# A third block's rounded weights in a place of their own, ahead of the up projection of a hybrid decoder step

## The reference, cut to what matters

```python
def conv_ffn(x, buf, w_up, conv_w, conv_b, w_down):
    h_gate, h_val = jnp.split(x @ w_up, 2, axis=-1)
    hc, new_buf = causal_dwconv(h_gate, buf, conv_w)
    return (jax.nn.silu(hc + conv_b) * h_val) @ w_down, new_buf

# for each layer l
h = h + gt_m * rmsnorm(out, p['norm_g'][l, 1])              # behind the token mixer
u = rmsnorm(h, p['norm_g'][l, 2]) * (1 + sc_f) + sh_f       # ahead of the channel mixer
out, nb = conv_ffn(u, st_conv_f[l], p['ffn_w_up'][l], ...)
```

## Time and profile before

| | us |
|---|---|
| median of 3 runs | 3021.64 |
| lowest, highest | 3018.35, 3023.63 |
| span of the profiled execution, first to last instruction | 3014.3 |
| PE busy in it | 2876.1 (95%) |
| DVE, ACT, POOL busy in it | 1528.4, 1085.0, 1321.5 |

### The profile page before, as it was taken

One profiled execution on the slowest core, in us unless ns is written; L12 is line 12 of the kernel. 1 busy time (PEld: TensorE's weight loads), 2 busy tenths in 40 slices (PEclk: granted clock), 3 DMA queues, 4 the chain that ended last, 5 costly groups with the idle time before them and its releaser, 6 DMA issues.

```text
span 3014.3 us, 72962 instructions
## 1 busy us (share of the span) xinstructions
PE 2876.1 (95%) x29617; PEld 2733.3 (91%) x29617; DVE 1528.4 (51%) x2080; ACT 1085.0 (36%) x2139; POOL 1321.5 (44%) x959
## 2 busy tenths in 40 slices
PE   6999999998989999999998999999999999899998
PEld 5998999997978877899997899889999899799998
DVE  3435666118357874666603242476650444566612
ACT  4224333225455652433323444343332422433322
POOL 3443444442435554344443273434444344344443
PEclk9999999999999999999999999999999999899999
DMA  7544333544411013333354323533334543133332
GB/s 269 164 151 159 95 92 88 158 128 136 119 44 32 4 37 124 120 89 92 99 159 152 99 64 112 169 123 89 92 116 146 173 120 91 57 92 92 91 91 85
DMA packets 465618, 332.56 MB, mean 110 GB/s; under 512 B 19914, under 2 KB 435608, under 8 KB 465122
## 3 DMA queue, kind: packets, MB, share of 16 engines
q1 hardware_dynamic: 461400, 325.24, 35.1%
q10 hardware_dynamic: 4010, 4.22, 0.6%
HBM read 319.62 MB, written 10.20 MB: 109 GB/s over the span
## 4 chain that ended last, share of the span: by engine, by line
PE 62%; DVE 4%; ACT 2%; issue 1%; DMA 1%; SPq 0%; POOL 0%; ACTq 0%; DVEq 0%
PE banks L1667 33%; PE banks L1675 16%; PE banks L2126 5%; PE banks L2133 1%; PE banks L1628 1%; PE banks L1973 1%; DVE h L2662 1%; PE banks L1690 1%; DVE proj L2606 1%; PE banks L1761 0%; DMA s_state<-in_state_wkv_b_dram 0%; ACT conv L1080 0%; PE banks L2135 0%; ACT uv L1433 0%; DVE proj_b L2606 0%
## 5 line engine op out<-in xcount | busy, mean ns | idle before, releaser
L765 POOL TENSOR_TENSOR w_lo<-w_raw,w_hi 128x1024 fp32r<-128x1024 f32 x395 | 1007.5, 2551 | 1108.1 <-ACT w_hi L981 1088.0
L1667 PE MATMUL banks<-u_hi,w_hi 128*128 128x260 f32 x4064 | 834.5, 287 | 14.2 <-ACT w_hi L981 9.4
L1667 PE MATMUL banks<-u_lo,w_hi 128*128 128x260 f32 x4064 | 825.1, 284 | 0.0
L1667 PEld LDWEIGHTS banks<-u_hi,w_hi 128*128 128x128 f32 x4064 | 627.4, 189 | 27.1 <-issue 15.2
L1667 PEld LDWEIGHTS banks<-u_lo,w_hi 128*128 128x128 f32 x4064 | 629.9, 189 | 1.6
L981 ACT ACTIVATE w_hi<-w_raw 128x1024 fp32r<-128x1024 f32 x402 | 424.5, 1056 | 454.2 <-PE banks L1675 284.4
L1675 PE MATMUL banks<-u_hi,w_lo 128*128 128x260 f32 x4064 | 527.5, 282 | 0.0
L1675 PEld LDWEIGHTS banks<-u_hi,w_lo 128*128 128x128 f32 x4064 | 502.1, 187 | 1.3
L1667 PE MATMUL banks<-hid_hi,w_hi 128*128 128x260 f32 x1664 | 336.3, 283 | 0.0
L1667 PE MATMUL banks<-hid_lo,w_hi 128*128 128x260 f32 x1664 | 335.2, 283 | 0.0
L3113 DVE TENSOR_TENSOR csb<-proj 128x520 f32 (+1 forms) x42 | 30.3, 722 | 470.8 <-ACT proj L1048 470.8
(11 more groups left out here) (463 smaller groups left out, 3898.8 us busy)
## 6 DMA issues: line engine op xcount, KB each, us to landing
w_raw<-in_ffn_w_up_dram SPq DMA_DIRECT2D x176, 512.0 KB, 3.7
ada_raw<-in_ada_w_dram SPq DMA_DIRECT2D x96, 512.0 KB, 4.7
w_raw<-in_ffn_w_down_dram SPq DMA_DIRECT2D x64, 448.0 KB, 3.7
w_raw<-in_sconv_w_in_dram SPq DMA_DIRECT2D x48, 512.0 KB, 5.2
ada_ahead<-in_ada_w_dram SPq DMA_DIRECT2D x36, 512.0 KB, 7.7
ada_ahead_down<-in_ada_w_dram SPq DMA_DIRECT2D x36, 512.0 KB, 6.2
w_raw<-in_ffn_w_down_dram SPq DMA_DIRECT2D x32, 512.0 KB, 4.0
ada_pro<-in_ada_w_dram SPq DMA_DIRECT2D x6, 2048.0 KB, 21.2
```

The lines of the kernel that those rows point to most:

```text
L765: pool.tensor_tensor(w_lo[:, s, :, :], w_raw[:, s, :, :], w_hi[:, s, :, :].bitcast(F32), ALU.subtract).then_inc(lo_done, 1)
L1667: pe.matmul(tile_ps[slot][half][0:width, 0:HALF], w_hi[:, s, k, 0:width], x[:, k0 + k, half * HALF:(half + 1) * HALF], start=start and k = ...
```

## The change

The rounded part of the up projection's third block (block `n0 + 2`, the second unit's gate) goes to a place of its own, `third_hi`, instead of slot 0 of `w_hi`. So its rounding need not wait until the first pair has been multiplied: ACT does it in the norm behind the mixer, right behind the second block's rounding. There it waits for the third block's load (`w_loaded[0]`). PE multiplies the third block with `third_hi`; the transposes of the first unit's tail and of the second unit's state move from ahead of this block into it, between its 32 and its 16 matmuls. The load of the Silu table moves behind the first gate's copies. POOL makes the third block's rest from `third_hi`, once the first pair is done (`low_third`). On ACT and POOL the loop's first round is written out.

```diff
--- before.py
+++ after.py
@@ -230,6 +230,7 @@
         wa2 = at("wa2", [8, 2, GH * P], F32, half_off + 2 * T * 4)
         shift_rows = at("shift_rows", [NSEQ, D], F32, big_off + 3 * slab_bytes)
         shift_in = at("shift_in", [NS, D], F32, half_off)
+        third_hi = at("third_hi", [P, KT, P], F32R, big_off + 37440)
         ahead_at = {0: [big_off + 62400 + i * 4 * ADA_W for i in range(6)],
                     2: [big_off + 3 * slab_bytes + 8192 + i * 4 * ADA_W for i in range(6)],
                     "down": [u_off + slab_bytes + i * 4 * ADA_W for i in range(4)]
@@ -765,6 +766,13 @@
                 pool.tensor_tensor(w_lo[:, s, :, :], w_raw[:, s, :, :], w_hi[:, s, :, :].bitcast(F32),
                                    ALU.subtract).then_inc(lo_done, 1)
 
+            def low_third(n):
+
+                pool.wait_ge(hi_done, n + 1)
+                pool.wait_ge(block_done, n + 1)
+                pool.tensor_tensor(w_lo[:, 0, :, :], w_raw[:, 0, :, :], third_hi[:, :, :].bitcast(F32),
+                                   ALU.subtract).then_inc(lo_done, 1)
+
             def low_parts(n, s):
 
                 pool.wait_ge(hi_done, n + 1)
@@ -941,7 +949,11 @@
                         if ahead:
                             low(n0 + 4 * it + 2 * e + 3, 1)
 
-                    with pool.Fori(0, p["iters"] - 1) as it:
+                    tails(q0, 0, gate_ready)
+                    low_third(n0 + 2)
+                    low(n0 + 3, 1)
+                    hidden_tile(0, 1, True)
+                    with pool.Fori(1, p["iters"] - 1) as it:
                         hidden_tile(it, 0, True)
                         hidden_tile(it, 1, True)
                     hidden_tile(p["iters"] - 1, 0, True)
@@ -1087,6 +1099,9 @@
                     if n0 < NBLK:
                         half_of = lambda _n: n0 // 2
                         high(n0 + 1, 1)
+                    if p["sub"] == 1:
+                        act.wait_ge(w_loaded[0], 16 * (n0 // 2 + 1) + 16)
+                        act.activation(third_hi[:, :, :], w_raw[:, 0, :, :], ACT.Copy).then_inc(hi_done, 1)
                 elif p["kind"] == "sconv":
                     j = l // 3
 
@@ -1521,9 +1536,7 @@
                     out_pair(p["iters"] - 1, True)
                 elif p["kind"] == "up":
 
-                    act.activation(warm[:, :], eps_col[:, :], ACT.Silu)
-
-                    def hidden_tile(it, e, ahead):
+                    def hidden_tile(it, e, ahead, first=False):
 
                         nonlocal half_of
                         n, q, m = n0 + 4 * it + 2 * e, q0 + 2 * it + e, 2 * it + e
@@ -1538,7 +1551,10 @@
                         act.wait_ge(gate_ready, q + 1)
                         act.sem_inc(tile_free[0], 1)
                         half_of = lambda _n: n0 // 2 + 2 * it + e + 1
-                        high(n + 2, 0)
+                        if first:
+                            act.activation(warm[:, :], eps_col[:, :], ACT.Silu)
+                        else:
+                            high(n + 2, 0)
                         act.wait_ge(conv_done, q + 3)
                         act.activation(conv[:, e, 0:CWD], conv[:, e, 0:CWD], ACT.Silu,
                                        bias=vec("ffn_conv_b", l * FT + m)).then_inc(silu_done, 1)
@@ -1548,7 +1564,9 @@
                                      O["conv_ffn_prompt"][l, 0, :, ds(m * P, P)],
                                      O["conv_ffn_sample"][l, :, 1, ds(m * P, P)])
 
-                    with act.Fori(0, p["iters"] - 1) as it:
+                    hidden_tile(0, 0, True, True)
+                    hidden_tile(0, 1, True)
+                    with act.Fori(1, p["iters"] - 1) as it:
                         hidden_tile(it, 0, True)
                         hidden_tile(it, 1, True)
                     hidden_tile(p["iters"] - 1, 0, True)
@@ -1656,15 +1674,16 @@
                     pe.wait_ge(ada_pro_loaded[i % KT], 16 * (2 * (h - 2) + i // KT + 2))
                     ada_columns(ahead_of(h)[i % KT][:, :], i % KT)
 
-            def gemm(n, s, slot, xh, xl, k0, nk, start, stop, ready=None, width=P, between=None):
+            def gemm(n, s, slot, xh, xl, k0, nk, start, stop, ready=None, width=P, between=None, high=None):
 
                 pe.wait_ge(hi_done, n + 1)
+                stationary = w_hi[:, s] if high is None else high
                 for k in range(nk):
                     if ready is not None:
                         pe.wait_ge(ready[0], ready[1] + k + 1)
                     for i, x in enumerate((xh, xl)):
                         for half in range(2):
-                            pe.matmul(tile_ps[slot][half][0:width, 0:HALF], w_hi[:, s, k, 0:width],
+                            pe.matmul(tile_ps[slot][half][0:width, 0:HALF], stationary[:, k, 0:width],
                                       x[:, k0 + k, half * HALF:(half + 1) * HALF],
                                       start=start and k == 0 and i == 0, stop=False)
                 if between is not None:
@@ -2445,14 +2464,23 @@
                             pe.wait_ge(tile_free[0], t0 // 2 + 1)
                             pe.wait_ge(tile_free[1], t0 // 2 + 1)
                             gemm_pair(n0, p["pre"], u_hi, u_lo, (u_ready, KT * (p["split"] - 1)))
-                        else:
-                            for part in range(2):
-                                pe.wait_ge(tile_free[part], t0 // 2 + 2 * it + e + 1)
-                                gemm(n0 + 4 * it + 2 * e + part, part, part, u_hi, u_lo, 0, KT, True, True)
+                            return
+                        for part in range(2):
+                            pe.wait_ge(tile_free[part], t0 // 2 + 2 * it + e + 1)
+                            gemm(n0 + 4 * it + 2 * e + part, part, part, u_hi, u_lo, 0, KT, True, True)
                         turn_tail(q, e)
 
+                    def second_states():
+
+                        turn_tail(q0, 0)
+                        turn_state(q0 + 1, q0 // 2, 1)
+
                     hidden_tile(0, 0, True)
-                    hidden_tile(0, 1)
+                    pe.wait_ge(tile_free[0], t0 // 2 + 2)
+                    gemm(n0 + 2, 0, 0, u_hi, u_lo, 0, KT, True, True, between=second_states, high=third_hi)
+                    pe.wait_ge(tile_free[1], t0 // 2 + 2)
+                    gemm(n0 + 3, 1, 1, u_hi, u_lo, 0, KT, True, True)
+                    turn_tail(q0 + 1, 1)
                     with pe.Fori(1, p["iters"]) as it:
                         for e in range(2):
                             hidden_tile(it, e)
```

## The result

The changed kernel takes 3039.32 us (median of 6 runs, 3038.09 to 3048.40); the kernel before, measured beside it, takes 3019.42 (6 runs, 3015.76 to 3023.63). The ratio is 1.0071, with a 95% interval of 1.0060 to 1.0082: slower, by about 20 us. The forecast was 3046, its range 3036 to 3060.

The account below looks back on a forecast made before the run. PE, busy 2876.1 of 3014.3 us, was taken as the bound, so its idle and half clock decide. 31.3 + 1.5 - 4.8 - 3.4 = +24.6 us gave span 3038.9 and time 3046 us, range 3036 to 3060.

Parts of the forecast that it names:

- The wait: Norm ahead of up, layers 0 to 2: rounding waits for its load ahead of the squares, delaying the root; +31.3 us.
- The clock behind the root: Layers 0 to 2, spreading or first pair after the root: part may run at half clock; 0.5 a layer, +1.5 us.
- The rival of a clock that stays low through the first pair: Layers 0 to 2: idle leaves PE at half clock into the pair; some 3059 us, chance 0.15.
- the rival with the load in time: Third block's weights land when ACT is free, so no wait; four starts gain 8.2 us: 3013 us, chance 0.04.
- The gap: PE idle between first pair and third block shrinks: 1.3 us in layers 0 to 2, 0.9 in layer 3; -4.8.
- Hidden by 0.2 us only: Up start: fourth block's wait for the first unit's product stays covered by 0.2 us; otherwise a few tenths per layer.
- Layer 3: Its third-block load lands some 3.7 us after issue, before the first square, so the wait costs nothing there.
- The half clock behind the gap: Third block's beginning, two of four layers: half clock gone with the shorter gap; -3.4 us.
- The median: Whole kernel: forecast span 3038.9, with the earlier median's 7.3 us above its span added, gives 3046 us.

Follow-up runs that it names:

- the wait alone: Kernel before plus ACT waiting for the third block's load where the change rounds it, nothing rounded early: 3045.28 us against 3017.74, ratio 1.0088.
- the earlier load: Changed kernel with SP issuing the third block's load ahead of the eight `ada_w` loads: 3013.65 us, ratio to the kernel before 0.9984.
- the rounding behind the root: Changed kernel with the third block's rounding moved behind the root of the norm ahead of the channel mixer, load unmoved: 3009.45 us, ratio 0.9971.
- without the own place: Changed kernel with the third block rounded into slot 0 behind the pair again, ahead of the table's load, transposes still inside the block: 3022.27 us.
- the rest in its own place: Changed kernel with the third block's load issued earlier, plus POOL making the block's rest in `third_lo` behind the root: 3011.01 us, ratio to before 0.9976.
- the second execution: The changed kernel run once more, unchanged: 3046.73 us, against 3017.67 for the kernel before beside it.
- the table alone: Kernel before with only the Silu table's load moved, behind the third block's rounding: 3016.86 us, one run.

## Why the prediction was right

**The wait** was the largest term and decided the sign. It was put at +31.3 us of root delay; the table gives 9.05 + 12.98 + 9.82 = 31.9, and the wait alone, in the kernel before, loses 27.5 us in the end; the earlier load wins 31.6 back in the four places and some 26 in the whole kernel. Two errors cancel in it: the squares could begin 1.3 us sooner in sum than I had them (the load landed 9.0 us behind its issue in layer 0, not 10.0), and from square to root it took 8.0, 9.4 and 8.5 us, where I had 8.0 in each and 9.3 as the upper bound. The 9.4 is layer 1, whose sums stay longest at the half clock.

**The clock behind the root.** The size agrees by luck: +1.5 predicted, +1.65 found (+1.3 with a pair that is 0.35 us shorter), but all of it in layer 1, where the `ada_w` columns behind the root run at the half clock. The kernel with the rounding behind the root and the one without the own place show the same 6.33 us in the same layer, and neither has the long idle ahead of it. So no run shows that the idle caused this part. First a round of layer 1, then of layer 0:

```profile
1250.48 1.93 PE L1646 MATMUL banks<-ada_ahead,cT 128*32 128x256 f32 x16
```

```profile
285.93 1.07 PE L1646 MATMUL banks<-ada_ahead,cT 128*32 128x256 f32 x16
```

What the long idle does show is the low clock of the sums. The clock that falls over an idle stretch agrees with what the Trainium skill says (TensorE: Matmul & The Clock Gate, "What's actually happening"): 0.65 over the 11.8 idle us, then 0.50 under work.

**The rival of a clock that stays low through the first pair** is wrong: PE is at 0.81 in the mean before the root already, and the pair takes 12.1 us in layers 0 and 2, as it did. Of the rival with the load in time, the mechanism was right, only not for this kernel: with the load ahead there is no wait, and the time is 3013.65 us. That it had 3013 is luck: it took 8.2 us off 3021.64, and the gain measured against the kernel before beside it is 4.1 us (3017.74 to 3013.65).

**The gap** was put at -4.8 us and the half clock behind it at -3.4, together -8.2. From the pair's end to the fourth block it was 9.75, 9.76, 8.24 and 7.81 us and is 6.98 in each: -7.65; the fourth block is 0.08 longer in each, which leaves -7.3. Within this the gap is shorter than I had it (0.63, not 0.9 to 1.0: the gate's copies begin at 299.80, ahead of the end of the pair's last products at 300.01), and the third block longer: 6.35, not 6.0.

**"Hidden by 0.2 us only"**, of the fourth block behind the first product, is the step that failed. The product ends 6.2 us behind the gate's copies, as it did (6.13). But the third block begins 0.1 us behind them, not 0.3, and its own 6.06 us then end ahead of product and signal. I had also counted no signal: the fourth block starts 0.23 us behind the product's end. It costs 0.3 us a layer. That the product is no sooner, though nothing stands ahead of DVE, has the cause that the kernel with the rest in its own place shows: one of DVE's three steps always runs beside POOL's rest. In the kernel before it was the third one; DVE and POOL there:

```profile
292.43 2.65 DVE L2578 SCALAR_TENSOR_TENSOR conv<-gate,vecs,conv 128x536 f32<-128x536 f32 x1 [0.15 <-DVE conv L2576]
```

```profile
292.08 2.43 POOL L765 TENSOR_TENSOR w_lo<-w_raw,w_hi 128x1024 fp32r<-128x1024 f32 x1 [0.68 <-ACT w_hi L981]
```

**Layer 3** was to be free and is: 2.3 us shorter than before. Only some 0.8 of this belongs to the gap and the blocks behind it. The root is 0.8 us earlier and the pair 0.7 shorter, which I had not forecast; the root repeats in the second execution, the pair doesn't (14.45 us), and this layer is then 0.85 us shorter than before. So it is in part luck that the four places come to +24.3 us where the sum had +24.6; in the second execution they come to +26.6.

**The half clock behind the gap** went in both layers, as predicted, but my reason was too simple. Over all executions it followed none of the 28 gaps of 0.63 to 1.56 us. Of the gaps of 1.9 to 2.4 us it followed 2 of 4 in the kernel before, the same two when repeated, 2 of 4 without the own place, and none with the wait alone or the table alone. It repeats within a kernel and is not set by the gap's length. What sets it stays open.

**The median** came out 6.7 us below the 3046. By the spans the step is +22.9 where my sum was +24.6, which is 1.7 of it. The rest, 5 us, is the way from the span to the time: I added 7.3 us, the distance of the first median from the span shown. But the changed kernel's profiled execution took 3038.95 us, 1.75 more than its span, and the kernel before, profiled once more, took 3017.32, 2.1 more than its span of 3015.2; so most of the 7.3 was that the execution shown of before happened to be a short one. That was no property of the kernel and should not have been carried over in full. By the medians the step is +19.9 us, and in the later pair of single runs +29.1 (3046.73 against 3017.67), so the scatter of executions is as large as this miss. The upper end of the forecast's own range, 3056, was also not its bounds' sum: 3014.3 + 39.2 + 7.3 is 3060.8.

## What to carry to other kernels

Before an instruction is moved forward in an in-order queue, look up two things in the trace: when the data that it waits for lands, and what stands behind it in the queue. Here a 1 us rounding was moved in front of the squares that all of the next stage hangs on, while its load stood behind eight others; the same rounding behind the root, or the same load eight places earlier, took the loss away and made the kernel 0.1 to 0.3% faster than before instead of 0.7% slower. And a gap of which several pieces are to go is worth only what the next limit allows: of 1.8 us of gap in layer 2, 1.3 came out, since the product of another engine set the start of the block after.

## What the runs showed of the hardware

- A DVE step of 128x536 with three operands took 0.78 us alone and 2.65 or 2.82 us beside a subtraction on POOL that had begun 0.35 or 0.14 us sooner. In both cases it ended 0.57 us behind POOL's end (295.08 against 294.51, 304.17 against 303.60). The kernel before has 208 such steps. 102 of them lasted 2.64 to 2.99 us, and all of these ran beside POOL's rest and ended 0.57 to 0.58 us behind its end; the other 106 took 0.78, most of them begun 0.3 to 0.6 us ahead of POOL's instruction. That is a step held up until POOL is done, not one that runs at a lower rate. The Trainium skill says so (SBUF — State Buffer, "SBUF: two separate sides"): the two share a port pair as an exclusive lock, which a DVE operation with two on-chip inputs needs against a GpSimd operation that reads there. If all of the step's 0.78 us came behind the lock, it would end 0.78 us behind POOL, which is an estimate; here it was 0.57.
- The Silu table's load took 1.28 us (300.64 to 301.92 in the changed kernel); ACT stood idle 0.10 us ahead of it, and the next ACT instruction stood 0.01 us behind it.
- A load of 512 KB behind eight others landed 8.9 to 10.0 us after its issue, in layers 0 to 2 of the kernel before and of the changed one. With nothing ahead of it, in layer 3 of the kernel before, the same load took 3.7 us, which is also the median of all 176. While it was under way in layer 0 of the changed kernel, the DMA engines were at 0.97 and moved 357 GB/s.
- The half clock came without a long idle too. In layer 1 of the kernel without the own place, eight sums took 0.44 us at 1222.78 (0.68 is the half clock), and 16 matmuls of `ada_w` columns took 1.92 us at 1235.04, where they take 1.07 at the full clock. PE's longest idle in between is 1.5 us.
